# One key block of the first attention: high and low parts of the meta keys in one set of rows

## The reference, cut to what matters

```python
decay = fq[:, :, :, None] - fk[:, :, None, :]          # cumulative log-forget values
logits = einsum('bqhd,bkhd->bhqk', q, k) * DH ** -0.5 + decay
logits = where(mask, logits, NEG)
p = softmax(logits, axis=-1)
o = einsum('bhqk,bkhd->bqhd', p, v)
```

## Time and profile before

| | |
|---|---|
| median of 3 runs | 1333.79 us (1332.71 to 1335.61) |
| the profiled execution, span | 1335.2 us |
| PE busy | 1282.8 us (96%) |
| DVE, ACT, POOL busy | 708.4 us (53%), 435.8 us (33%), 529.0 us (40%) |

### The profile page before, as it was taken

The page is one execution under the profiler, slowest core; times in us unless marked ns, Lnnn a source line. Parts: engine busy times, 40 slices in busy tenths (PEclk is TensorE's granted clock), DMA queues, the critical chain, the costliest instruction groups (busy, mean ns, idle before and its releaser), DMA issues. The chain is left out here.

```text
span 1335.2 us, 21499 instructions
## 1 busy us (share of the span) xinstructions
PE 1282.8 (96%) x8573; PEld 1241.7 (93%) x8573; DVE 708.4 (53%) x1368; ACT 435.8 (33%) x843; POOL 529.0 (40%) x580
## 2 busy tenths in 40 slices
PE   6999999999999999999999999999999999999996
PEld 6999999999999999989999999889999999998996
DVE  7466462446344453565334488356665666566145
ACT  6323232223222232343114233234443444335111
POOL 2344343525162525153666656502123122237522
PEclk9999999999999999999999999889999999999998
DMA  5231212222121211033413148802212311214412
GB/s 214 93 102 56 77 56 74 75 76 67 57 96 44 94 52 64 25 152 125 168 67 113 52 106 293 253 9 67 58 28 66 74 50 30 66 57 173 153 51 82
DMA packets 54515, 120.65 MB, mean 90 GB/s; under 512 B 12416, under 2 KB 29440, under 8 KB 54160
## 3 DMA queue, kind: packets, MB, share of 16 engines
q1 hardware_dynamic: 51696, 110.24, 24.8%
q0 software_dynamic: 2432, 8.78, 2.5%
q10 hardware_dynamic: 288, 0.26, 0.1%
HBM read 80.57 MB, written 35.89 MB: 87 GB/s over the span
## 5 line engine op out<-in xcount | busy, mean ns | idle before, releaser
L83 PE MATMUL psum<-act,fox_slot_hi 128*128 128x358 f32 (+1 forms) x552 | 183.2, 332 | 10.3 <-DVE act L988 10.3
L84 PE MATMUL psum<-act,fox_slot_hi 128*128 128x358 f32 (+1 forms) x552 | 180.3, 327 | 0.0
L85 PE MATMUL psum<-act,fox_slot_lo 128*128 128x358 f32 (+1 forms) x552 | 180.0, 326 | 0.0
L1314 POOL TENSOR_SCALAR fox_rows<-fox_f_keys,fox_f_query 128x144 f32<-128x144 f32 (+3 forms) x64 | 50.3, 786 | 177.1 <-PE psum L692 174.1
L83 PEld LDWEIGHTS psum<-act,fox_slot_hi 128*128 128x128 f32 x552 | 104.4, 189 | 10.4 <-DVE act L988 10.3
L84 PEld LDWEIGHTS psum<-act,fox_slot_hi 128*128 128x128 f32 x552 | 104.3, 189 | 0.0
L85 PEld LDWEIGHTS psum<-act,fox_slot_lo 128*128 128x128 f32 x552 | 104.2, 189 | 0.0
L878 ACT ACTIVATE fox_pT_hi<-psum 128x512 fp32r<-128x512 f32 (+3 forms) x112 | 52.3, 504 | 103.8 <-PE psum L692 103.8
L856 ACT ACTIVATE fox_rows<-fox_rows,fox_neg_max 128x144 f32<-128x144 f32 (+3 forms) x64 | 50.6, 791 | 97.1 <-DVE fox_neg_max L1069 96.2
L83 PE MATMUL psum<-fox_slot_hi,act 128*128 128x256 f32 (+1 forms) x288 | 81.1, 282 | 0.0
L85 PE MATMUL psum<-fox_slot_hi,act 128*128 128x256 f32 (+1 forms) x288 | 81.0, 281 | 0.0
(11 more groups left out here) (400 smaller groups left out, 3963.7 us busy)
## 6 DMA issues: line engine op xcount, KB each, us to landing
fox_x<-in_xT SPq DMA_DIRECT2D x8, 536.0 KB, 9.7
out<-fox_key SPq DMA_DIRECT2D x8, 536.0 KB, 2.7
mix_resid<-in_xT SPq DMA_DIRECT2D x8, 536.0 KB, 3.8
resid_b<-mix_resid SPq DMA_DIRECT2D x8, 536.0 KB, 2.9
q_nope<-mla_nope SPq DMA_DIRECT2D x8, 536.0 KB, 4.9
mla_query<-q_nope SPq DMA_DIRECT2D x8, 536.0 KB, 5.1
mla_end_y<-resid_b SPq DMA_DIRECT2D x8, 536.0 KB, 6.7
fox_f_keys<-f_cum SPq DMA_DIRECT2D x8, 520.0 KB, 4.2
```

The costliest lines, as they stand in the source:

```text
L83: pe.matmul(out, lh, rh, start=start and k == 0, stop=False)
L84: pe.matmul(out, lh, rl, start=False, stop=False)
L85: last = pe.matmul(out, ll, rh, start=False, stop=stop and k == n - 1)
L1314: chain(pool.tensor_scalar(row[:, KEY_META:KEY_META + live], f_keys[h % 2][:, 0:live], 1.0, f_query[:, i + 1, h:h + 1], ALU.mult, ALU.add))
```

## The change

Block 0 has 112 rows without a key. After the change, its four quarters of 32 rows carry the 16 meta keys in their upper halves: DVE writes the meta probabilities, times the reciprocal, three more times into columns 16 to 31, 48 to 63 and 80 to 95 of the row, and leaves columns 112 to 127 as they are. After the transpose, ACT rounds block 0 as before; DVE then replaces its partitions 64 to 127 by the low part. A new tile `value_meta`, zero elsewhere, holds the high part of the meta values in rows 16 to 31 and 80 to 95 and the low part in rows 48 to 63, so that one pass adds hi hi, lo hi and hi lo. Three transfers on POOL's queue, of 16 rows of 1 KB each, fill it once for each pair of heads. `pT_lo` of block 0 is no longer written or read.

```diff
+def meta_copies(a):
+    return a[:, 0:3 * P // 4].rearrange("p (a b) -> p a b", a=3)[:, :, P // 4 - N_META:P // 4]
+def meta_thrice(a):
+    return a[:, P - N_META:P].rearrange("p (a b) -> p a b", a=1).to_broadcast([P, 3, N_META])
...
+        value_meta = sb("value_meta", [P, 2 * DH], F32R)
...
+        meta_zeroed, meta_loaded = sem("meta_zeroed"), sem("meta_loaded")
...
                 cols = slice(DH * (h % 2), DH * (h % 2) + DH)
+                if h % 2 == 0 and j == 0:
+                    pe.wait_ge(meta_loaded, 48 * (h // 2) + 48)
+                pe.matmul(O[:, 0:2 * P], value_meta[:, cols], pT_hi[:, 0, :], start=True, stop=False)
                 three_pass(pe, O[:, 0:2 * P], [(value_hi[:, k, cols], value_lo[:, k, cols], pT_hi[:, k, :], pT_lo[:, k, :])
-                                               for k in range(2 * j + 3)]).then_inc(out_full, 1)
+                                               for k in range(1, 2 * j + 3)], start=False).then_inc(out_full, 1)
...
                 act.wait_ge(proj_full[b], nth + 1)
+                if p and t == 0:
+                    act.wait_ge(meta_loaded, 48 * p)
                 act.activation(value_hi[:, t, :], PJ[b][:, 0:2 * DH], ACT.Copy, scale=rms_rows[:, t:t + 1]).then_inc(value_rounded, 1)
...
                 dve.wait_ge(inv_done, n + 1)
-                row = rows[n % 3][:, first:first + used]
+                inv = row_inv[:, n % 4:n % 4 + 1]
+                dve.tensor_scalar(meta_copies(rows[n % 3]), meta_thrice(rows[n % 3]), inv, None, ALU.mult)
+                row = rows[n % 3][:, P:first + used]
                 dve.tensor_scalar(row, row, row_inv[:, n % 4:n % 4 + 1], None, ALU.mult).then_inc(probs_ready, 1)
...
                     dve.wait_ge(turn_rounded, split_turns.at[(h, i, g)] + 1)
-                    dve.tensor_tensor(pT_lo[:, k:k + n, cols], PT[b][:, 0:P * n].rearrange("p (a b) -> p a b", b=P),
-                                      pT_hi[:, k:k + n, cols].bitcast(F32), ALU.subtract).then_inc(turn_split, 1)
+                    if k == 0:
+                        half = slice(P // 2, P)
+                        dve.tensor_tensor(pT_hi[half, 0, cols], PT[b][half, 0:P], pT_hi[half, 0, cols].bitcast(F32), ALU.subtract)
+                    s = 0 if k else 1
+                    dve.tensor_tensor(pT_lo[:, k + s:k + n, cols], PT[b][:, P * s:P * n].rearrange("p (a b) -> p a b", b=P),
+                                      pT_hi[:, k + s:k + n, cols].bitcast(F32), ALU.subtract).then_inc(turn_split, 1)
...
                 pool.wait_ge(value_taken, v + 1)
+                if p and t == 0:
+                    pool.wait_ge(meta_loaded, 48 * p)
...
+            def load_meta(p):
+                v = value_order.at[("V", p, 0)]
+                pool.wait_ge(value_rounded, v + 1)
+                pool.wait_ge(value_split, v + 1)
+                if p:
+                    pool.wait_ge(out_full, out_use(2 * p - 1, 3) + 1)
+                else:
+                    pool.wait_ge(meta_zeroed, 1)
+                for n in range(3):
+                    to, src = P // 4 * n + P // 4 - N_META, value_lo if n % 2 else value_hi
+                    pool.dma_start(value_meta[to:to + N_META, :], src[P - N_META:P, 0, :]).then_inc(meta_loaded, 16)
...
             job("G", 0)
+            pool.memset(value_meta[:, :].bitcast(F32), 0.0).then_inc(meta_zeroed, 1)
...
                 low_values(0, t)
+            load_meta(0)
             job("K", 1)
...
                             low_values(use[1], use[2])
+                        if use[0] == "V" and use[2] == 0:
+                            load_meta(use[1])
```

## The result

| | before | after |
|---|---|---|
| median | 1334.75 us (1332.71 to 1336.94, 6 runs) | 1340.97 us (1338.28 to 1343.80, 6 runs) |
| ratio of after to before | | 1.0054, 95% interval 1.0038 to 1.0070 |
| profiled execution, span | 1335.2 us | 1336.5 us |

The change makes the kernel 6.2 us (0.5%) slower; 4.2 us faster was forecast. The profiled execution of after is the fastest of its six runs (1338.28 us; its span, from the first instruction to the last, is 1.8 us less than its time). By the same 1.8 us, an estimate, the span of before's, 1335.2, belongs to a time of 1337.0, about the slowest of its six (1336.94). So the two traces, 1.3 us apart, show less of the difference than the medians. They are read here for where the time goes, not for how much in all.

The account below looks back on a forecast made before the run. PE was taken to bound the kernel up to the last head, DVE's chain there. -6.7 (passes) + 2.1 (waits) + 1.4 (last head) - 1.0 (ahead of head 0) = -4.2 us: 1329.6 us, range 1325.7 to 1334.3.

Parts of the forecast that it names:

- the last head: Six multiplications and six splits lengthen DVE's chain by 1.6 us; passes saved at the end give 0.24; net +1.4 us.
- Removed passes: Value products lose 64 matmuls of 0.12 us each, 7.7 us in all, 6.7 of it in heads 0 to 6.
- The half split: On DVE ahead of the wide split: without overlap, the end of each pair of splits comes 0.15 us later.
- the two waits on a bank: PE's transposes at i = 3 and i = 5 wait 0.15 us longer in each of 7 heads: +2.1 us.
- the 0.66 of the prediction: Heads 1 to 6 become shorter by about 0.66 us each (0.96 - 0.30), or the forecast fails.
- The multiplication: Ahead of each rescale on DVE, 0.12 us; hidden by PE's projections in heads 1 to 6, paid in the last head.
- second rival: Last head: the multiplication uses up DVE's turn, so the rescale waits for POOL's next instruction, +2.4 us a hit; chance 0.20.
- Ahead of head 0: Issuing transfers delays POOL's weight splits, freeing DVE's earlier steps; PE's 1.25 us wait goes; counted as -1.0 us.
- Transfers in the loop: Later pairs' transfers fit POOL's idle time and land before PE needs them, 13.7 us after issue; counted as nothing.
- third rival: Small transfers land late and PE stands at a pair's first product; 6.9 us lost at 16 us, 1336.5 us; chance 0.05.
- The later stages move with PE: Behind the attention the same instructions start behind a barrier of all engines and move with PE; no change counted.

Follow-up runs that it names:

- e1: Kernel before with only the 64 passes for block 0 taken out; no transfers, copies or half split: 1328.07 us, -7.1.
- e2: Changed kernel without the copies and the half split, so passes taken out and transfers on POOL's queue: 1332.26 us, -2.9 against before.
- e4: e2 with the half split added, the multiplication still left out: 1336.27 us, +1.2 against before.
- f4: Kernel before, all three passes kept, with the transfers on POOL's queue added and their rows not read: 1336.97 us, +2.2.
- g3: Kernel before with a DVE multiplication of 48 columns of zeros added ahead of each rescale: 1339.67 us, +5.5.
- f1: Changed kernel with the transfers on SP's queue instead of POOL's: 1337.10 us, +2.3 against before.
- f3: Changed kernel with two passes for block 0 in place of the half split, transfers on SP's queue: 1336.98 us, +2.2 against before.
- g1: Changed kernel with the copies by ACT instead of DVE's multiplication and the transfers on SP's queue: 1335.39 us, +1.2 against before.
- f2: e2 with the transfers on SP's queue instead of POOL's: 1328.79 us, -6.0 against before.
- g2: Changed kernel with two passes instead of the half split, copies by ACT, transfers on SP's queue: 1333.56 us, -0.6 against before.
- e3: e2 with DVE's small multiplication added, the half split still left out: 1335.55 us, +0.4 against before.
- g4: Changed kernel with the copies by ACT instead of DVE's multiplication, transfers left on POOL's queue: 1337.44 us, +3.3 against before.

## Why the prediction was wrong

Along e1, e2, e4 and after, each kernel adds one part to the last, so the four steps sum to +6.2 us. The prediction's sum, in the same parts:

| part | predicted | measured |
|---|---|---|
| 64 passes | -6.7 - 0.2 = -6.9 | -7.1 |
| transfers | -1.0 | +4.2 (f4 alone: +2.2) |
| half split | +2.1 + 0.9 = +3.0 | +4.0 |
| multiplication | +0.7 | +5.1 (on e2: +3.3; g3 alone: +5.5) |
| sum | -4.2 | +6.2 |

In the two traces the parts of the way compare so: ahead of head 0 -1.0 us was forecast and -1.0 came; heads 0 to 6 -4.6 and 0.0; the last head +1.4 and +1.3; behind the attention nothing and +2.7. So what the forecast missed lies in heads 0 to 6 and behind the attention.

**Removed passes: right.** 0.12 us each. Of the 6.7 us due in heads 0 to 6, 5.8 arrive in e1; the rest is mostly the new wait for the query's split in heads 1, 3 and 5.

**The half split: mechanism right, a wait missed.** Nothing overlaps (the wide split starts 0.31 us behind the half one), and the two waits on a bank grow as worked out: gap by gap in heads 1 to 6 of e4, by 0.17 and 0.18 us, against 0.15. Heads 2, 4 and 6 of e4 have nothing else new and are 0.6 us shorter than before, near the 0.66 of the prediction. By the Trainium skill (VectorE: DVE Perf Modes, Two Vector instructions with no wait between them) that absence of overlap was to be expected between operands that start in different groups of 32 partitions, and the rows here agree. Left out was who else stands behind the splits in DVE's order: the query's split at i = 6 of the odd heads, 3 waits of up to 0.6 us with the split alone, 0.8 in after.

**The multiplication: this step failed.** "In heads 1 to 6 the rescale is followed by projections on PE, which hide it" put its cost there at nothing and priced it by its length in the last head. Its length is nearly right (0.25 us, 0.17 to the next start, against 0.12), but that isn't what it costs. First, the projections hide the rescale only from the transposes that read it. They do not hide it from the splits that stand behind it in DVE's order, and PE's waits hang on those splits: from e4 to after, 2.2 us more in heads 0 to 6, where nothing was forecast, half of it in head 0. Second, it is one more DVE instruction per block that POOL can hold, and behind a held one the next POOL instruction comes up in time to hold the rescale too. The prediction had this second point as its second rival, with the right place, for the last head alone, and gave it 0.20 in all and 0.07 for two hits or more. The argument against it, that POOL's next instruction comes up some 0.1 us too late, was wrong where POOL works back to back: in f1, L1390 starts 0.03 us ahead of the rescale. Three of the traces show that pair of holds at i = 6 of the last head (f1, f3, g3: rescales of 2.94 to 2.95 us); after's own shows the smaller one at i = 5, while the hold that before has at i = 6 (1.79 us) is absent there (0.67), so that its last head comes out as forecast partly by luck. By the Trainium skill (GPSIMD Engine Reference, Key points) the two engines share SBUF interfaces, with contention where the DVE instruction runs in a two-port mode or has two SBUF inputs. The trace of f1 agrees that the two engines get in each other's way, with 1.06 + 2.94 us instead of 0.25 + 0.67; in which mode the rescale runs, no run here shows.

Such a hold may cost clock as well. In f3's trace PE waits for the held rescale, and 1.5 us after that wait the granted clock is at half, the 1.2 GHz level, for 3.4 us (a line of the timeline and one of the windows):

```profile
596.83 1.09 PE L719 MATMUL psum<-ident,fox_rows 128*128 128x128 f32 x8 [1.83 <-DVE fox_rows L1114]
...
598.00:602.00 4.00, 3.96 (x15) 3.65 (x16) 2.98 (x6) 2.20 (x4) 2.15 (x1) 0.57 0.00 0
```

In the last head of all other traces the clock stays up, in f1's and g3's too, which have the same pair of holds; so this is seen once and not shown as a rule.

**Ahead of head 0: right in size.** -1.03 us, and PE's L641 starts with no wait, as forecast for L629. All six kernels with the transfers on POOL's queue gain 1.0. But it can be had without them: of the kernels that issue nothing on POOL's queue, f1, g1 and g3 gain 1.4 there, while e1, f2, f3 and g2 gain nothing and show the old wait of 1.25.

**Transfers in the loop: right.** They land 1.7 to 2.9 us after issue and nobody waits; the third rival falls.

**"The later stages move with PE": this step failed.** The barrier stands between the first and the last product of the second layer's latents. That stretch takes 76.7 to 77.3 us in five of the six profiled kernels with transfers on POOL's queue (e2, e3, after, f4, g4; 75.4 in e4) and 75.1 to 75.7 in the eight others. In after it is 77.04 against 75.49, 1.55 us more: PE's wait is 1.0 longer, the products at half clock cost 1.3 (they start 0.30 us apart instead of 0.16), and a wait of 0.7 us for DVE that before had 12 us later is gone. PE's wait at the barrier is 2.0 to 2.6 us in those five, 1.9 in e4 and 1.5 to 1.6 in the eight; the stretch at half clock right behind it is in those five traces and in none of the others. From the last value product to the end, the means are 729.1 us (the six) and 727.3 (the eight), 1.8 apart; single executions scatter more, and g2's, with nothing on POOL's queue, is the longest with 730.4. The three pairs that differ in the queue alone give 3.1, 3.9 and 2.1 us by their medians.

The clock tells the same of all runs, not only of the profiled ones, since each run has its mean granted clock on record. Averaged over the runs it is 0.9895 in e2, 0.9890 in after and 0.9901 in g4, and 0.9916, 0.9920 and 0.9923 in their partners f2, f1 and g1; before has 0.9918 to 0.9924. Over 1336 us these differences come to 2.8, 4.0 and 2.9 us of full clock. That is an estimate of the most that they can cost, since PE is not busy all the time, and it is about what the three pairs lose. f4 alone of the six is no lower (0.9918, and 0.9921 beside it), though its trace shows the stretch at half clock; that would fit its lower price, if most of its other runs kept the clock, but no trace of those shows it. That the DRAIN grows when POOL's queue has carried transfers is shown; why, no run here shows.

**What stays open.** The traces of before and after differ by 3.0 us from the first value projection on, the medians by 6.2. Of the multiplication's 5.1 us they place 3.0, of g3's 5.5 they place 2.5. Some of the rest may be clock: g3's runs have 0.9911 on the average and those of before beside them 0.9924, at most 1.7 us; that is not shown. The last head took 31.0 us in after's trace and 33.0 in f1's, with the same DVE work, so executions of one kernel may differ there too; which of them the unprofiled runs took isn't recorded. Each step of the table is uncertain by some 2.4 us. And the prediction set the span of the profiled execution (1335.2) against a median of times; like with like it stands about 3.2 us above the median, not 1.4. The forecast goes from the median and does not depend on this.

## What to carry to other kernels

Price a small instruction on an engine that another engine can hold not by its length alone: see what the other engine runs at that moment, and whether its next instruction is ready when the small one ends; where the chain has no cover, give the extra work to an engine that is not held (ScalarE here, with 0.24 to 0.25 us for each of its copies). Before the first transfer goes onto a queue that has carried none in that part of the program, look at what the next barrier does with that queue, and at what the clock does after the pause. And look at everything that stands behind a lengthened instruction in its engine's order, and at who waits for that, not only at the reader of its own result.

## What was not expected of the hardware

- 12 transfers of 16 KB on POOL's queue make POOL's DRAIN at the next barrier 1.0 us longer, 3.50 to 3.52 us against 2.51 to 2.53, though the last of them was issued 211 us earlier (497.6 against 708.5 us).
- PE's first value projection starts between 38.55 us (after) and 41.08 us (f4), in no order that follows the changes: 2.5 us of difference between profiled executions that no change here explains. A pair of profiles can't be compared by their spans alone.
- A DVE instruction of 72 columns ahead of head 0 (before's L1208) takes 2.42 to 2.44 us beside a POOL subtraction of 1024 columns or 0.97 beside a POOL rounding, and the stretch to head 0 then takes 57.5, 56.5 or 56.1 us.
